# Deferring the RMS normalisation at three borders into feed-forward stages of a two-block transformer kernel

## What is computed

```python
h = rms_norm(x, norm_g[layer, 2]) * (1.0 + scale[:, :, 2]) + shift[:, :, 2]
x = x + 0.5 * gate[:, :, 2] * swiglu(h, ffn_w_in[layer, 1], ffn_w_down[layer, 1])

def rms_norm(h, gain):
    h32 = h32 * lax.rsqrt(jnp.mean(h32 * h32, axis=-1, keepdims=True) + EPS)
    return (h32 * gain.astype(jnp.float32)).astype(h.dtype)

def swiglu(h, w_in, w_down):
    a, b = jnp.split(h @ w_in, 2, axis=-1)
    return (jax.nn.silu(a) * b) @ w_down
```

## Time and profile before

| | us |
|---|---|
| median of 3 runs | 2413.76 (2407.76 to 2414.72) |
| profiled execution, own time | 2414.24 |
| its span | 2412.6 |
| granted TensorE clock, mean of the span | 0.994 |
| PE busy | 2379.7 (99%) |
| DVE busy | 1273.3 (53%) |
| ACT busy | 861.0 (36%) |

### The profile page before, as it was taken

The page is one execution under the profiler, slowest core; times in us unless marked ns, Lnnn a source line. Parts: engine busy times, 40 slices in busy tenths (PEclk is TensorE's granted clock), DMA queues, the critical chain, the costliest instruction groups (busy, mean ns, idle before and its releaser), DMA issues.

```text
span 2412.6 us, 30397 instructions
## 1 busy us (share of the span) xinstructions
PE 2379.7 (99%) x11034; PEld 1906.3 (79%) x11034; DVE 1273.3 (53%) x1953; ACT 861.0 (36%) x1320; POOL 202.5 (8%) x337
## 2 busy tenths in 40 slices
PE   7999999999999999999999999999999999999998
PEld 5888888677788888888888888888888888867766
DVE  6886334455678873343333355555533333459654
ACT  4232223566543222242222243344422222344453
POOL 1212000000002110000000013331000000020200
PEclk9999999999999999999999999999999999999999
DMA  8899332321259973223333321212233333232211
GB/s 279 281 289 286 110 96 73 97 62 53 70 170 290 285 228 108 86 79 96 96 99 108 89 79 53 62 53 79 85 99 96 96 110 96 66 95 66 61 53 53
DMA packets 420385, 285.27 MB, mean 118 GB/s; under 512 B 22690, under 2 KB 397788, under 8 KB 420304
## 3 DMA queue, kind: packets, MB, share of 16 engines
q1 hardware_dynamic: 397888, 207.64, 29.8%
q0 software_dynamic: 20896, 73.80, 9.2%
q10 hardware_dynamic: 1520, 2.77, 0.3%
HBM read 281.85 MB, written 6.72 MB: 120 GB/s over the span
## 4 chain that ended last, share of the span: by engine, by line
PE 92%; DVE 3%; ACT 2%; DMA 1%; issue 1%; SPq 1%; POOL 0%; ACTq 0%; DVEq 0%; POOLq 0%
PE bank L685 13%; PE bank L687 13%; PE bank L686 13%; PE bank L860 7%; PE bank L862 7%; PE bank L861 7%; PE bank L1529 4%; PE bank L1531 4%; PE bank L1530 4%; PE bank L1556 2%; PE bank L720 2%; PE bank L722 2%; PE bank L721 2%; PE bank L1178 1%; PE bank L1151 1%; PE bank L700 1%
## 5 line engine op out<-in xcount | busy, mean ns | idle before, releaser
L641 DVE TENSOR_TENSOR w_lo<-raw,w_hi 128x1024 fp32r<-128x1024 f32 (+1 forms) x331 | 434.1, 1312 | 427.3 <-ACT w_hi L622 421.8
L622 ACT ACTIVATE w_hi<-raw 128x1024 fp32r<-128x1024 f32 (+1 forms) x331 | 369.7, 1117 | 482.5 <-PE bank L687 242.9
L685 PE MATMUL bank<-h_hi,w_hi 128*128 128x512 f32 x1344 | 523.0, 389 | 1.1 <-DVE w_lo L641 1.1
L687 PE MATMUL bank<-h_hi,w_lo 128*128 128x512 f32 x1344 | 522.8, 389 | 0.0
L686 PE MATMUL bank<-h_lo,w_hi 128*128 128x512 f32 x1344 | 522.8, 389 | 0.0
L685 PEld LDWEIGHTS bank<-h_hi,w_hi 128*128 128x128 f32 x1344 | 252.3, 188 | 54.3 <-DVE w_lo L641 2.0
L686 PEld LDWEIGHTS bank<-h_lo,w_hi 128*128 128x128 f32 x1344 | 252.3, 188 | 52.4
L687 PEld LDWEIGHTS bank<-h_hi,w_lo 128*128 128x128 f32 x1344 | 252.3, 188 | 52.1
L860 PE MATMUL bank<-g_hi,w_hi 128*128 128x512 f32 x704 | 277.8, 395 | 0.0
L862 PE MATMUL bank<-g_hi,w_lo 128*128 128x512 f32 x704 | 276.0, 392 | 0.0
L861 PE MATMUL bank<-g_lo,w_hi 128*128 128x512 f32 x704 | 273.2, 388 | 0.0
(11 more groups left out here) (420 smaller groups left out, 3020.5 us busy)
## 6 DMA issues: line engine op xcount, KB each, us to landing
raw<-in_ffn_w_in SPq DMA_DIRECT2D x176, 512.0 KB, 4.0
ada<-in_ada_w POOLq DMA_DIRECT2D x128, 512.0 KB, 5.0
raw<-in_ffn_w_down SPq DMA_DIRECT2D x64, 704.0 KB, 4.6
raw<-in_hgrn_w_in SPq DMA_DIRECT2D x32, 512.0 KB, 4.0
raw<-in_attn_w_qkv SPq DMA_DIRECT2D x24, 512.0 KB, 3.8
raw<-in_w_in SPq DMA_DIRECT2D x22, 512.0 KB, 3.8
ada_first<-in_ada_w SPq DMA_DIRECT2D x16, 512.0 KB, 10.7
bias_scratch<-bias_lines POOLq DMA_DIRECT2D x14, 320.0 KB, 9.0
```

Source lines behind the costliest of these rows:

```text
L622: line(nc.scalar.activation(w_place(n, 0, k * P)[0], raw[:, n % 4, 0:k * P], ACT.Copy), hi_ready)
L641: line(nc.vector.tensor_tensor(lo, raw[:, n % 4, 0:k * P], hi.bitcast(F32), ALU.subtract), lo_ready)
L685: nc.tensor.matmul(out_ap, wh, xh, start=(k == 0), stop=False)
L687: last = nc.tensor.matmul(out_ap, wl, xh, start=False, stop=end)
```

## The change

At the borders m = 2, 3 and 5 (into F1, F2 and F3) norm_pe with its idle turns goes. In the stage before, after each new tile of x, ACT writes u_hi = xT * scale_col into h_hi and DVE u_lo into h_lo; scale_col is computed ahead of that part. All eight squares are added to sumsq by DVE. PE multiplies the first two blocks with u, one after the other (deferred_pair), with one product of ones and sumsq behind the third tile. Then the true h is written over u for the blocks from the third on, in the order of deferred_norm_act and deferred_norm_dve. DVE multiplies banks 0 and 1 by rstd. The part of the shift is a column for each block: DVE adds up the raw weights of both blocks, each tile times its shift (shift_sum_dve, eight operations over 128x256), PE sums the result over the partitions with two one-column products, and it goes in as the bias of Silu and as the scalar of the product with it. The splits of the fourth and fifth block move; sumsq is cleared after the first four blocks.

```diff
+        DEFERRED = (2, 3, 5)
+        U_AT = {2: {3: (0, 1), 4: (2, 3), 5: (4, 5), 6: (6,), 7: (7,)}}
...
+        def u_hi_act(act, line, m, j, i=None):
+            for k in u_tiles(m, j):
+                xj, hi, _, scale = u_parts(k, i)
+                line(nc.scalar.activation(hi, xj, ACT.Copy, scale=scale), uhi_ready)
+        def u_lo_dve(dve, line, m, j, i=None):
+            for k in u_tiles(m, j):
+                dve.wait_ge(uhi_ready, plus(i, 2, KD * deferred_before(m) + k + 1))
+                xj, hi, lo, scale = u_parts(k, i)
+                line(nc.vector.scalar_tensor_tensor(out=lo, in0=xj, scalar=scale, in1=hi.bitcast(F32), op0=ALU.mult,
+                                                    op1=ALU.subtract), ulo_ready)
...
+        def shift_sum_dve(dve, line, m):
+            n = FIRST[NEXT[m]]
+            assert n % 4 == 0
+            acc = tmp[:, 3, 0:2 * P].rearrange("p (b n) -> p b n", n=P)
+            for b in range(2):
+                dve.wait_ge(landed[n % 4 + b], landings(n + b))
+            for k in range(KD):
+                tiles = raw[:, 0:2, k * P:(k + 1) * P]
+                s = mod[:, 24 * m + k:24 * m + k + 1]
+                line.settle()
+                if k == 0:
+                    line(nc.vector.tensor_scalar(acc, tiles, s, None, ALU.mult))
+                else:
+                    line(nc.vector.scalar_tensor_tensor(out=acc, in0=tiles, scalar=s, in1=acc, op0=ALU.mult, op1=ALU.add),
+                         shift_sum if k == KD - 1 else None)
+        def deferred_pair(pe, m, banks):
+            n, d = FIRST[NEXT[m]], deferred_before(m)
+            pe.wait_ge(shift_sum, d + 1)
+            for b in range(2):
+                last = nc.tensor.matmul(B[4][:, b:b + 1], tmp[:, 3, b * P:(b + 1) * P], ones[:, 0:1], start=True,
+                                        stop=True)
+            last.then_inc(shift_ps, 1)
+            for b in range(2):
+                s = (n + b) % 2
+                pe.wait_ge(x_ready, KD * m + KD - 1 + b)
+                pe.wait_ge(lo_ready, n + b + 1)
+                for k, (uh, ul) in enumerate(H_TILES):
+                    if b == 0:
+                        pe.wait_ge(ulo_ready, KD * d + k + 1)
+                    wh, wl = w_hi[:, s, k * P:(k + 1) * P], w_lo[:, s, k * P:(k + 1) * P]
+                    nc.tensor.matmul(banks[b][:, :], wh, uh, start=(k == 0), stop=False)
+                    nc.tensor.matmul(banks[b][:, :], wl, uh, start=False, stop=False)
+                    last = nc.tensor.matmul(banks[b][:, :], wh, ul, start=False, stop=(k == KD - 1))
+                    if k == KD - 1:
+                        last.then_inc(used, 1)
+                    elif b == 1:
+                        last.then_inc(u_used, 1)
+                    elif k == KD // 2 - 1:
+                        last.then_inc(half_used, 1)
+                    if b == 0 and k == 2:
+                        pe.wait_ge(sum_full, d + 1)
+                        nc.tensor.matmul(B[5][:, :], ones[:, :], sumsq[:, :], start=True, stop=True).then_inc(rms_ps, 1)
+        def deferred_norm_act(act, line, m, after):
+            n, d = FIRST[NEXT[m]], deferred_before(m)
+            norm_root_act(act, line, m)
+            for j in range(KD):
+                if j < KD - 1:
+                    act.wait_ge(u_used, (KD - 1) * d + j + 1)
+                else:
+                    act.wait_ge(used, n + 2)
+                act.wait_ge(t_ready, KD * m + j + 1)
+                line(nc.scalar.activation(h_hi[:, j, :], tmp[:, j % 4, :], ACT.Identity,
+                                          bias=mod[:, 24 * m + j:24 * m + j + 1]), hhi_ready)
+                if j == 1:
+                    first_half_hi(act, line, m)
+                elif j == 2:
+                    split_hi(act, line, n + 2)
+            split_hi(act, line, n + 3)
+            if after:
+                nc.scalar.preload_act_table(after)
+        def deferred_norm_dve(dve, line, m):
+            n, d = FIRST[NEXT[m]], deferred_before(m)
+            line(nc.vector.tensor_scalar(gate_col[:, :], mod[:, 24 * m + 16:24 * m + 24],
+                                         1.0 if m % 3 == 1 else 0.5, None, ALU.mult))
+            dve.wait_ge(shift_ps, d + 1)
+            line(nc.vector.tensor_copy(shift_col[:, :], B[4][:, 0:2]), shift_col_ready)
+            dve.wait_ge(rstd_ready, m + 1)
+            def lower(j):
+                dve.wait_ge(hhi_ready, KD * m + j + 1)
+                line(nc.vector.scalar_tensor_tensor(out=h_lo[:, j, :], in0=tmp[:, j % 4, :],
+                                                    scalar=mod[:, 24 * m + j:24 * m + j + 1],
+                                                    in1=h_hi[:, j, :].bitcast(F32), op0=ALU.add,
+                                                    op1=ALU.subtract), h_ready)
+            for j in range(KD):
+                if j >= 4:
+                    dve.wait_ge(h_ready, KD * m + j - 3)
+                line(nc.vector.scalar_tensor_tensor(out=tmp[:, j % 4, :], in0=xT[:, j, :],
+                                                    scalar=scale_col[:, j:j + 1], in1=rstd[:, :],
+                                                    op0=ALU.mult, op1=ALU.mult), t_ready)
+                if j:
+                    lower(j - 1)
+                if j == 3:
+                    first_half_lo(dve, line, m)
+                elif j == 4:
+                    split_lo(dve, line, n + 2)
+            lower(KD - 1)
+            split_lo(dve, line, n + 3)
+            for b in range(2):
+                dve.wait_ge(used, n + b + 1)
+                line(nc.vector.tensor_tensor(B[b][:, :], B[b][:, :], rstd[:, :], ALU.mult), unscaled)
...
+            m = stage_after(n)
+            if m in DEFERRED:
+                dve.wait_ge(sq_ready, line.value(x_ready))
+                line(nc.vector.tensor_tensor(sumsq[:, :], sumsq[:, :], sq[:, :], ALU.add),
+                     sum_full if j == KD - 1 else sum_ready)
+                u_lo_dve(dve, line, m, j, i)
+                if j == KD - 1:
+                    split_lo(dve, line, n + 2)
+                    line.settle()
+                return
...
+            if stage_after(n) in DEFERRED:
+                u_hi_act(act, line, stage_after(n), j, i)
...
-                        product(pe, n + 2 * s + b, B[2 * s + b][:, :], H_TILES, i)
+                        fresh = (h_ready, KD * NORM_OF[name] + 1) if b == m == 0 and NORM_OF[name] in DEFERRED else None
+                        product(pe, n + 2 * s + b, B[2 * s + b][:, :], H_TILES, i, waits=fresh)
...
+                late = NORM_OF[name] in DEFERRED and m == 0
                 for s in range(2):
-                    if m or s:
+                    if (m or s) and not late:
                         split_hi(act, line, n + 2 * s + 1, i)
-                    split_hi(act, line, n + 2 * s + 2, i)
+                    if not late:
+                        split_hi(act, line, n + 2 * s + 2, i)
                     f0 = KF * fidx + 2 * m + s
-                    act.wait_ge(used, plus(i, 4, n + 2 * s + 1))
+                    if late and s == 0:
+                        act.wait_ge(unscaled, 2 * deferred_before(NORM_OF[name]) + 1)
+                    else:
+                        act.wait_ge(used, plus(i, 4, n + 2 * s + 1))
                     if f0:
                         act.wait_ge(gt_ready, plus(i, 2, f0))
-                    line(nc.scalar.activation(sq[:, :], B[2 * s][:, :], ACT.Silu), silu_ready)
+                    if late and s == 0:
+                        act.wait_ge(shift_col_ready, deferred_before(NORM_OF[name]) + 1)
+                        line(nc.scalar.activation(sq[:, :], B[0][:, :], ACT.Silu, bias=shift_col[:, 0:1]), silu_ready)
+                        split_hi(act, line, n + 4)
+                    else:
+                        line(nc.scalar.activation(sq[:, :], B[2 * s][:, :], ACT.Silu), silu_ready)
...
+                    if late and s == 0:
+                        dve.wait_ge(unscaled, 2 * deferred_before(NORM_OF[name]) + 2)
+                        line(nc.vector.scalar_tensor_tensor(out=tmp[:, 0, :], in0=B[1][:, :], scalar=shift_col[:, 1:2],
+                                                            in1=sq[:, :], op0=ALU.add, op1=ALU.mult), gt_ready)
+                        split_lo(dve, line, n + 4)
+                    else:
+                        line(nc.vector.tensor_tensor(tmp[:, s, :], sq[:, :], B[2 * s + 1][:, :], ALU.mult), gt_ready)
...
+            if NORM_OF[name] in DEFERRED:
+                line(nc.vector.memset(sumsq[:, :], 0.0))
+                line.settle()
...
                     split_lo(dve, line, n + 2 * s + 1, i)
+                    if m and s and RES_OF[name] in DEFERRED:
+                        shift_sum_dve(dve, line, RES_OF[name])
                     split_lo(dve, line, n + 2 * s + 2, i)
                     residual_dve(dve, line, n + 2 * s + 1, 2 * m + s, i)
...
```

(26 more changed lines are left out.)

35 lines of the change are left out of this document (31 added, 4 removed).

## The result

| | before | after |
|---|---|---|
| median, 6 runs each | 2412.98 us (2407.76 to 2414.72) | 2420.59 us (2418.99 to 2422.12) |
| profiled execution, span | 2412.6 | 2417.2 |
| last osq product of the attention to the sumsq product ahead of P2 | 1452.79 | 1459.70 |

The ratio is 1.0033, 95% interval 1.0023 to 1.0043: 7.6 us slower by the medians, where 2.0 was forecast. The forecast's 2415.8 was 4.8 short, inside its range of 2408 to 2422. But "no measurable change", less than 7.2 us, was called likeliest, and what came is a loss: by the interval it lies between 5.5 and 10.4 us. That it is a loss is clear of the noise; that it passes 7.2 is not.

A forecast was written before the change was run, and what follows sets the result against it. PE was taken to bound the kernel, busy 2379.7 of 2412.6 us. F2 -1.7, F1 4.2 - 1.7 = +2.5 and F3 2.9 - 1.7 = +1.2 gave +2.0 on 2413.76: 2415.8 us, range 2408 to 2422.

The forecast's parts named there:

- The shift sum: Ahead of the last WO and HO blocks: eight chained DVE operations take 4.05 us, with ends 3.1 and 6.3.
- estimate of 3.1 us: Low bound for the eight DVE shift operations, if waiting on the one before costs nothing extra; total then +0.1, 2413.9.
- Rival D: Shift operations in WO and HO take 6.3 us instead of 4.05: total +6.6, 2420.4; 0.75 together with the forecast.
- The waits: PE waits for DVE's splits before late blocks: WO loses 1.2 and 3.05, together 4.2 us, HO 2.9.
- The borders: Into F1, F2, F3: idle turns go, DVE's third-block work takes most back; block four ends at T + 26.3, gain 1.7 each.
- sumsq product: PE's product with finished sumsq, behind three tile products of the first block at each border, taken as 0.86 us.
- F1's seventh block: DVE's memset and ada sums use up 0.6 us before its split; loss taken as zero, bound 0.5.
- The clock: PE's new pauses in WO, HO and third blocks may halve the clock; 3.4 us a fall, kept out of the sum.
- two falls: Two drops to 1.2 GHz after PE's new pauses: total +8.8, 2422.6, slower than the bound; chance 0.14 for two or more.
- the prediction's own sign: Prediction wrong if third-block waits are under 1 us, the sum over 5 or under 3, or the clock 0.5 behind 44 us.
- The range: Whole kernel 2408 to 2422 us: takes in 2413.9 and 2420.4, reaching towards the faster rival and the clock's fall.
- Rival B: Third block at each border does not wait for DVE and ACT: 4.9 us gained each, total -7.6, 2406.2; chance 0.11.

The follow-up runs named there:

- version with all parts: Against the kernel before: the change with its shift sum spread over idle DVE time, third-block tiles prepared early and sumsq's clearing moved; median 2404.45 us, ratio 0.9952.
- spread sum: Changed kernel with the eight shift operations put into DVE's idle time in WO and HO, WO's u tiles moved; median 2410.66 us, ratio 0.9991 to before.
- early preparation: Changed kernel with four scaled tiles and the first half split ahead of the third block's first h_lo; median 2411.62 us, ratio 0.9993 to before.

## Why the prediction came out as it did

**The shift sum: right.** Its operations on DVE in HO after:

```profile
1718.10 0.75 DVE L619 SCALAR_TENSOR_TENSOR h_lo<-xT,scale_col,h_hi 128x512 fp32r<-128x512 f32 x1
1718.99 0.35 DVE L641 TENSOR_SCALAR tmp<-raw,mod 128x256 f32<-128x256 f32 x1
1719.38 3.61 DVE L643 SCALAR_TENSOR_TENSOR tmp<-raw,mod,tmp 128x256 f32<-128x256 f32 x7
1722.90 1.22 DVE L787 TENSOR_TENSOR w_lo<-raw,w_hi 128x1024 fp32r<-128x1024 f32 x1
```

0.39 + 7 operations to 1722.90 is 3.91 us from the first start to the split (4.05 forecast), 0.50 to 0.52 a piece (0.525). The estimate of 3.1 us by the Trainium skill, VectorE: DVE Perf Modes, section on the DRAIN that can't be avoided, was not borne out; the row for chained operations, was the better guide. Rival D's 6.3 us is out as well: two pieces of raw cost nothing extra.

**The waits: right.** WO 1.2 and 3.05 forecast, together 4.2, and 4.5 measured, the 0.3 more ahead of block 6; HO 2.9 forecast, 3.0 measured. DVE's order from row to row was the right way to them. One sign was off: 2.5 to 3.5 us of waits were foreseen in the third and fourth blocks of each stage, and the view of waits has 1.0 for h_lo and 0.5 for w_lo at F2. What PE loses there is nearer to the forecast than what is counted as a wait: the third block of F2 starts at T + 12.62 and the fourth at T + 20.83, 8.2 us where a block lasts 5.45, since each of the waits has its re-entry behind it.

**The borders: right in mechanism, 0.25 too much each.** 1.7 forecast, 1.44 measured. The step that was mis-sized is the sumsq product: taken as 0.86 from the earlier trace rows, it cost 1.07 between two products with u, and the release of tile 0 came at T + 7.75 for 7.5. Everything behind moved by that.

**F1's seventh block: wrong.** "I take zero; bound 0.5", but it was 0.74. Timeline of DVE and PE in F1 after:

```profile
706.28 0.48 DVE L1261 MEMSET sumsq<- 128x512 f32 x1
707.06 1.23 DVE L787 TENSOR_TENSOR w_lo<-raw,w_hi 128x1024 fp32r<-128x1024 f32 x1 [0.29 <-DVE sumsq L1261]
...
713.36 1.22 DVE L787 TENSOR_TENSOR w_lo<-raw,w_hi 128x1024 fp32r<-128x1024 f32 x1
...
714.63 0.50 PE L850 MATMUL bank<-h_hi,w_hi 128*128 128x512 f32 x1 [0.42 <-DVE w_lo L787]
```

The memset was counted with its 0.48, but not the wait for its end, 0.29, that line.settle() puts behind it; with a re-entry of 0.4 that comes to 0.7. With the memset elsewhere, in the version with all parts, PE's wait of 0.42 went; the spread sum and the early preparation by themselves, which leave the memset in place, still have it, 0.43 and 0.45.

**The clock: the step that failed.** "The trace has one fall to the lower level: near 37 us" is false, and it was in the trace of before to be read. Windows of the kernel before:

```profile
2116.00:2117.00 1.00, 1.00 (x4) 0.79 (x3) 1.00 (x4) 0.00 (x0) 0.00 (x0) 0.50 0.30 50
2231.00:2239.00 8.00, 8.00 (x28) 5.75 (x28) 7.58 (x17) 1.08 (x2) 0.50 (x2) 0.57 0.00 0
2245.00:2249.00 4.00, 4.00 (x13) 3.12 (x13) 0.70 (x1) 2.20 (x4) 3.74 (x5) 0.57 0.00 0
```

The profile's row of tenths shows 9 in all 40 slices of 60 us and hides them. Read closer they give a price: 4 x 0.43 = 1.7 us, where the earlier trace rows and the stretch at 2231 lost twice as much. With it two falls would have given 2415.8 + 3.4 = 2419.2, under the bound of 7.2 us over before; and a chance of 0.14 for two falls was too low for pauses of nearly 3 us, which the trace of before didn't have anywhere behind the start, where its longest is 1.6. The rule of the Trainium skill, TensorE: Matmul & The Clock Gate, part on the clock gate, that idle stretches make the chip halve its clock, agrees with the falls in WO and HO. The other falls don't all follow it: in the 500 us ahead of the one at 2116 in the kernel before, PE has no pause of over 0.6 us, and right ahead of it no pause but small products. Timeline of PE:

```profile
2112.43 1.98 PE L2062 MATMUL bank<-z_ggate,w 16*128 16x512 f32 x4
2114.25 0.97 PE L2066 MATMUL bank<-ident,z_ggate 32*128 32x32 f32 x8
```

By the prediction's own sign, "if the clock is 0.5 anywhere behind 44 us", it was wrong. The sign was badly set, since the kernel before would have met it too.

**The range: luck.** The measured time lies in it, but not for the reason that set its upper end. Most of the room above the forecast was for a longer shift sum, 2420.4, and the sum was shorter than forecast. The clock, which was kept out of the sum, and F1's seventh block, which was taken as zero, filled that room.

**Rival B** (third block doesn't wait) did not happen: nine waits for h_lo, 2.9 us in all. The early preparation shows what it takes to bring it about, another order of the same instructions.

**The sum.** Forecast +2.0; missing were 3.0 of clock, 0.74 in F1, 3 x 0.25 at the borders and 0.4 in the waits: +6.9, the value of the sections. In the medians 0.7 more was seen, within their noise.

## What to carry to other kernels

Work that is taken off TensorE and put on VectorE is priced by where it stands in VectorE's order, not by its length: the same eight operations cost 9.8 us more in one piece ahead of a split than in the gaps that the engine already had (0.7 of that by the u tiles, which were moved with them). Where a pause of TensorE of nearly three microseconds or more is foreseen, allow for the clock too: here the fall behind it, where it came, cost about half of the pause again. And before a wait behind a long row of another engine is accepted, look for the idle stretch just ahead of that row: 2.08 us of it, filled, were worth 2.47 at each border.

## What was not expected of the hardware

- Losses of clock have few sizes. In the twelve traces of this case each stretch below full speed that starts between 30 and 2390 us lost 1.70 or 1.71 us, 3.41 or 3.42, or 5.12, and nothing in between. Some are in every trace (near 37 and near 2235 us), others come and go with the execution: 2116 in before, none there but one at 2209 and one at 2366 after. That goes with the spread of the runs of one kernel: of the kernel before, those with a granted clock of 0.996 took 2408 to 2410 us, those with 0.993 2414 to 2417, and 0.003 of its time is 7.2 us.
- Behind a single pause of PE between full streams of products, from 640 to 2100 us, the granted clock stayed at 1.00 in all eleven cases of 1.13 to 1.87 us. For 2.77 to 2.92 us it fell in three of four cases, for 3.68 and 3.83 us in both, once at twice the loss. What decides near 2.8 us is open: the same pause did and did not bring it. Between 1.87 and 2.77 us nothing was measured.
- The fall can come after the work has resumed: in the kernel with early preparation PE resumed at 670.68, the products at 670.99 and 671.22 still took 0.40 us, and the one at 671.69 took 0.62.
